# Values of two mixers computed in feature layout and turned by TensorE transposes, and a denominator summed in two fp32r parts

## The chip, the cores and the metric

The kernel runs on one core of one Trainium2 chip. The metric is the device time of one execution in microseconds (us), lower is better. Before the change the median of 3 runs is 1262.3 us (1262.03 to 1263.04).

## The reference

One layer of a decoder: 512 tokens and 16 learned meta tokens in front of them (528 in all), width 1024, all in float32. One input projection feeds three token mixers; this change touches the values of two of them and a denominator of the second.

```python
z = xn @ p["w_in"] + p["b_in"]          # 528 x 9696: q, k, v, r, a of GLA; DSA; q, k, v, o, i, f of mLSTM; gates
# GLA, 4 heads, keys 128 wide, values 256 wide, chunks of tokens:
o = einsum("bhtk,bhkv->bhtv", q * exp(G), S) + einsum("bhts,bhsv->bhtv", A, v)
# mLSTM, 4 heads, the same widths:
num = w_inter * einsum("bhtk,bhkv->bhtv", q, Cs) + einsum("bhts,bhsv->bhtv", P, v)
den = w_inter * einsum("bhtk,bhk->bht", q, ns) + sum(P, axis=-1)
h = num / maximum(abs(den), exp(-m))
# both: rms_norm per head, times a gate, then a projection to 1024
mix = sigmoid(gate_a) * y_a + sigmoid(gate_b) * y_b + sigmoid(gate_c) * y_c
h = h + rms_norm(mix @ p["w_out"], p["g_post_mix"])
h = h + rms_norm(square(relu(rms_norm(h, g) @ p["w_up"])) @ p["w_down"], p["g_post_mlp"])
```

## The kernel before

**Three products for one.** A product with a weight matrix is done on TensorE in the type fp32r. Activations and weights are split into a rounded part and a rest (`xh` and `xl`, `whi` and `wlo`), and three products are summed: high by high, high by low, low by high. A weight chunk is 1024 rows by 128 columns. SyncE loads it to one of three buffers `wraw`; GpSimd splits it to one of four buffers `whi`/`wlo` (L620, L624); TensorE uses it. `plan()` lists the chunks and the tiles that TensorE makes of them, in the order in which it makes them.

**Tiles and slots.** A tile of a product goes to one of two slots `GP` of PSUM, in turn. The next tile in a slot waits on the semaphore `gfree` until VectorE or ScalarE has copied the last one out. A tile in *feature layout* has its 128 channels on the partitions and the tokens along the free axis: the weight chunk is the stationary operand, the tokens stream. With `both=True` it covers all 528 tokens in two streams of 264 (L1871), otherwise 512 tokens (L1874). So 24 or 48 matmuls make a tile.

**Values before.** The mixers need values with tokens on the partitions. So the values of a head are made in *token layout*: 128 tokens are the stationary operand, and 256 columns of two weight chunks stream (L1889). Tile A has token tiles 0 and 1, tile B has 2 and 3, with 48 matmuls each. 16 tokens are left over: the first ones for GLA, the last ones for mLSTM. They are made in tile M by 16 matmuls (L1880, L1881), whose stationary operand `xm` holds the high and the low part of these tokens side by side in 32 columns. VectorE copies the tiles to `vh` (L1393) and `vm` (L1398) and adds the bias, which lies in `vb` on all partitions.

**Order of the work.** Every engine's queue is written out by hand. TensorE's main loop goes over the heads. Small steps of head h (`level`, `weighted`, `scores`, `recalled`, `squares`) stand between tiles for head h+1 (`nxt(...)`), so that TensorE has matrix work while VectorE and ScalarE prepare the next small step. In GLA the order per head is: tile gq of head h+1, `squares` of head h-1, gk, seven `level` steps with gg, gr, gr and A between them, the transposes of the keys (L2237, L2239), half of B, the state matmuls (L2244, L2247), the other half, M, `weighted` (L2188). In mLSTM it is: mq, `squares`, mq, `scores` 0 and 1 (L2285), mk, `scores` 2 and 3, A, `recalled` (L2293, L2294), the sum for the denominator, B, M. In the last head of each mixer, gate tiles (`ta`, `tc`) stand where the next head's tiles would.

**Denominator before.** VectorE adds the four weight blocks `AT` into `Wd` (L1697 to L1701, semaphore `sum_w`). TensorE multiplies a matrix of ones with `AT` for the first 112 columns (L2324) and with `Wd` for the other 400 (L2326), in plain fp32, which takes two instructions each. VectorE takes it up in `denominator` (L1707).

Of the kernel before, what the change touches and what calls it, by code (L numbers as in the profile page):

```python
# [69 lines left out]
def _rows():  # L70
    at = 0
    for name, n, src in [
        ("gq", 4, "b_in"), ("gk", 4, "b_in"), ("gr", 8, "b_in"), ("cq", 2, "b_in"), ("ckv", 1, "b_in"),
        ("ik", 1, "b_in"), ("mq", 4, "b_in"), ("mk", 4, "b_in"), ("mo", 8, "b_in"), ("gate", 24, "b_in"),
        ("a2", 4, "b_gla_a"), ("hg", 2, "g_gla_head"),
        ("hm", 2, "g_ml_head"), ("dq", 2, "g_dsa_q"), ("dkv", 1, "g_dsa_kv"), ("ig", 1, "idx_ln_g"),
        ("ib", 1, "idx_ln_b"), ("fb", 1, "ml_f_bias"), ("cv", 32, "ml_conv"),
    ]:
        ROWS[name] = at
        ROW_LIST.append((name, n, src))  # L80
        at += n
    return at
# [6 lines left out]
JOINED = {"gq": 8, "cq": 3, "mq": 8}  # L89
FOLLOWS = ("gk", "ckv", "mk")  # L90
# [21 lines left out]
NROWDMA = 22  # L112
# [22 lines left out]
def plan():  # L135
# [89 lines left out]
    def all_values(name, c0):  # L225
        pad()
        values(name, c0)

    gla(0)
    all_values("gv0", C_GV)  # L230
    for h in range(HEADS):
# [5 lines left out]
        if h + 1 < HEADS:  # L237
            all_values(f"gv{h + 1}", C_GV + (h + 1) * DV)
# [52 lines left out]
def build(nc, a, line, scratch, rows, out):  # L291
# [3 lines left out]
    with ctx:  # L295
# [6 lines left out]
        def region(offset, specs):  # L302
# [23 lines left out]
        xm = sb("xm", [P, KT, 2 * META], F32R)  # L326
# [44 lines left out]
        (sgate, gtmp, vb, qh, ATm, kh, vh, vm, AT, sqo, rso, on, km) = region(AO, [  # L371
            ("sgate", [P, 2, SEQ], FP32), ("gtmp", [P, 2, SEQ], FP32), ("vb", [P, D], FP32),
# [3 lines left out]
        BO = AO + (2 * SEQ * 2 + D + 2 * SEQ + 2 * ALL + 2 * QT * DV + 2 * DV + QT * SEQ + SEQ + 2 * SEQ + SEQ + 2 * SEQ + 2 * P) * 4  # L376
# [7 lines left out]
        (zc, cv, sgc, lf_, bcum_, M_, uT, uTt, fbias_, um_, Mb, Md, Wd, Mt, Wt, ATt, later_t) = region(BO, [  # L384
# [244 lines left out]
        def _(act):  # L629
# [41 lines left out]
            def input_high(t):  # L671

                if t == QT:
# [172 lines left out]
            act.dma_start(vb[:, :], a["b_in"][0:1, C_GV:C_GV + D].broadcast_to([P, D])).then_inc(ld_a, 16)  # L846
# [81 lines left out]

            gate_of(0)
            for h in range(HEADS):  # L930
                last = h == HEADS - 1
                level(h, 0)
                if h:
                    squared(h - 1)
                level(h, 1)
# [4 lines left out]
                level(h, 2)  # L940
                if last:
# [39 lines left out]
            act.dma_start(vb[:, :], a["b_in"][0:1, C_MV:C_MV + D].broadcast_to([P, D])).then_inc(ld_v, 16)  # L981
# [64 lines left out]
            fetch_maxima(0)  # L1046
            def head_squares(h):
# [10 lines left out]
            for h in range(HEADS):  # L1058
# [15 lines left out]
                floor_of(h)  # L1074
                if more:
# [7 lines left out]
                if more:  # L1083
                    conv_sig(h + 1, 1)
# [94 lines left out]
        def _(dve):  # L1179
# [45 lines left out]
            def input_low(t):  # L1225
                if t == QT:
# [3 lines left out]
                    dve.wait_ge(xl_ok, KT + 1)  # L1230
                    nc.vector.tensor_copy(xm[:, :, META:2 * META], xl[:, :, 0:META].bitcast(FP32)).then_inc(xl_ok, 1)
# [1223 lines left out]
```

## Time and profile before

| what | value |
|---|---|
| median of 3 runs | 1262.3 us |
| profiled execution, its own time | 1262.05 us |
| its span, first to last instruction | 1260.1 us |
| TensorE (PE) busy | 1252.5 us, 99%, 6561 instructions |
| VectorE (DVE) busy | 629.7 us, 50% |
| ScalarE (ACT) busy | 392.7 us, 31% |
| GpSimd (POOL) busy | 771.8 us, 61% |
| granted TensorE clock, mean | 0.999 |

The GLA heads run from about 345 to 560 us, the mLSTM heads from about 633 to 790 us of the span. The duration of a matmul in a row is from its start to its modelled end, and neighbours overlap: what a matmul costs is the distance from its start to the next start. In the table of groups a duration is a mean; in the timeline `xN` joins N neighbours that are alike.

### The profile page before, as it was taken

Reading aid. Unit: us, or ns where it says so; the run is one execution under the profiler, and the core shown is the slowest. Engines: PE = TensorE matmul, PEld = TensorE weight load, DVE = VectorE, ACT = ScalarE, POOL = GpSimd, SP = SyncE. Lnnn points to the kernel's source line nnn. Section 1 sums busy time; section 2 is a strip of 40 time slices with the busy share of each in tenths; the row PEclk is TensorE's granted clock in tenths of the full one; section 3 lists DMA queues with packets and bytes.
Section 4 is the critical chain, followed back from the end, with each engine's and each line's share of the span. In section 5 each row is a group of like instructions: output and inputs, shape, how many; then the busy total and the mean of one; then the engine's idle time right before and its main releaser. Section 6 shows DMA issues by size and latency. Waiting matters only on the chain.

```text
span 1260.1 us, 17438 instructions
## 1 busy us (share of the span) xinstructions
PE 1252.5 (99%) x6561; PEld 1028.6 (82%) x6564; DVE 629.7 (50%) x1115; ACT 392.7 (31%) x810; POOL 771.8 (61%) x914
## 2 busy tenths in 40 slices
PE   9999999999999999999999999999999999999998
PEld 8866887677899899888899987887888888888886
DVE  4368887642276786835446773342511112333434
ACT  5343555533013333333024343312511111221322
POOL 8746430225574753758775556784876676888882
PEclk9999999999999999999999999999999999999999
DMA  6846200323331321322443333522333333232221
GB/s 176 253 123 212 68 2 25 80 56 94 84 84 51 84 68 51 84 68 84 118 117 77 87 90 100 195 89 85 84 101 101 86 99 108 93 101 84 100 84 67
DMA packets 167433, 120.08 MB, mean 95 GB/s; under 512 B 11367, under 2 KB 145613, under 8 KB 167350
## 3 DMA queue, kind: packets, MB, share of 16 engines
q1 hardware_dynamic: 160612, 107.79, 29.7%
q10 hardware_dynamic: 6738, 11.18, 2.7%
q8 instruction: 52, 0.85, 0.3%
q14 instruction: 31, 0.25, 0.1%
HBM read 114.71 MB, written 9.62 MB: 99 GB/s over the span
## 4 chain that ended last, share of the span: by engine, by line
PE 99%; ACT 0%; DVE 0%; issue 0%; DVEq 0%; ACTq 0%
PE GP L1874 46%; PE GP L1910 9%; PE PA L1910 9%; PE GP L1889 7%; PE GP L1871 6%; PE PA L2075 3%; PE GP L2137 3%; PE PA L2175 1%; PE PA L2112 1%; PE PA L2293 1%; PE GP L2368 1%; PE GP L1956 1%; PE PA L2045 1%; PE PA L2285 1%; PE PA L2076 1%; PE GP L1881 1%
## 5 line engine op out<-in xcount | busy, mean ns | idle before, releaser
L624 POOL TENSOR_TENSOR wlo<-wraw,whi 128x256 fp32r<-128x256 f32 x708 | 563.9, 827 | 14.8
L620 POOL TENSOR_SCALAR whi<-wraw 128x1024 fp32r<-128x1024 f32 x177 | 201.0, 1135 | 449.2 <-PE GP L1874 226.6
L1874 PE MATMUL GP<-xh,whi 128*128 128x512 f32 x352 | 144.8, 411 | 0.0
L1874 PE MATMUL GP<-xh,wlo 128*128 128x512 f32 x352 | 139.0, 395 | 0.0
L1874 PE MATMUL GP<-xl,whi 128*128 128x512 f32 x352 | 138.8, 394 | 0.0
L1816 DVE TENSOR_TENSOR ul<-U,uh 128x512 fp32r<-128x512 f32 x64 | 65.3, 1055 | 109.4 <-ACT uh L1158 109.4
L1874 PE MATMUL GP<-nh,whi 128*128 128x512 f32 x240 | 95.1, 396 | 0.0
L1874 PE MATMUL GP<-nl,whi 128*128 128x512 f32 x240 | 95.1, 396 | 0.0
L1874 PE MATMUL GP<-nh,wlo 128*128 128x512 f32 x240 | 95.1, 396 | 0.0
L1820 DVE SCALAR_TENSOR_TENSOR U<-GP,rrow 128x512 f32<-128x512 f32 x32 | 22.1, 692 | 141.7 <-PE GP L1874 140.3
L1874 PEld LDWEIGHTS GP<-xh,whi 128*128 128x128 f32 x352 | 66.3, 188 | 16.0 <-issue 1.5
L1874 PEld LDWEIGHTS GP<-xh,wlo 128*128 128x128 f32 x352 | 66.1, 188 | 15.3
L1874 PEld LDWEIGHTS GP<-xl,whi 128*128 128x128 f32 x352 | 66.3, 188 | 14.3 <-issue 0.5
L1158 ACT ACTIVATE uh<-U 128x512 fp32r<-128x512 f32 x64 | 37.2, 625 | 129.0 <-PE PA L1910 70.4
L1874 PE MATMUL GP<-yh,whi 128*128 128x512 f32 x192 | 76.3, 397 | 0.0
L1874 PE MATMUL GP<-yl,whi 128*128 128x512 f32 x192 | 76.1, 396 | 0.0
L1874 PE MATMUL GP<-yh,wlo 128*128 128x512 f32 x192 | 76.1, 396 | 0.0
L1889 PE MATMUL GP<-whi,xh 128*128 128x256 f32 x256 | 74.6, 292 | 0.2 <-DVE kh L1404 0.2
L1889 PE MATMUL GP<-wlo,xh 128*128 128x256 f32 x256 | 71.9, 281 | 0.0
L1889 PE MATMUL GP<-whi,xl 128*128 128x256 f32 x256 | 71.7, 280 | 0.0
L1162 ACT ACTIVATE U<-U 128x512 f32<-128x512 f32 x32 | 20.2, 632 | 152.9 <-DVE U L1820 152.9
L1874 PEld LDWEIGHTS GP<-nh,wlo 128*128 128x128 f32 x240 | 45.2, 188 | 11.0
(426 smaller groups left out, 2770.5 us busy)
## 6 DMA issues: line engine op xcount, KB each, us to landing
wraw<-in_w_in SPq DMA_DIRECT2D x75, 512.0 KB, 3.9
wraw<-in_w_up SPq DMA_DIRECT2D x32, 512.0 KB, 4.0
wraw<-in_w_down SPq DMA_DIRECT2D x32, 512.0 KB, 3.5
line_rows<-bias_line SPq DMA_DIRECT2D x8, 655.0 KB, 5.2
table<-line_rows SPq DMA_DIRECT2D x4, 1024.0 KB, 5.7
wraw<-in_w_br_dsa SPq DMA_DIRECT2D x8, 512.0 KB, 4.3
wraw<-in_w_br_gla SPq DMA_DIRECT2D x8, 512.0 KB, 4.0
wraw<-in_w_br_ml SPq DMA_DIRECT2D x8, 512.0 KB, 4.0
```

The costliest lines, as they stand in the source:

```text
L620: nc.gpsimd.tensor_scalar(hi, src, 1.0, 1.0, ALU.mult, ALU.mult).then_inc(hi_done, 1)
L624: part = nc.gpsimd.tensor_tensor(lo[:, at:to], src[:, at:to], hi[:, at:to].bitcast(FP32), ALU.subtract)
L1158: nc.scalar.activation(uh[:, k % 4, :], U[:, k % FT, :], ACT.Copy).then_inc(uh_ok, 1)
L1162: nc.scalar.activation(U[:, m, :], U[:, m, :], ACT.Square).then_inc(U_ok, 1)
L1816: tt(ul[:, k % 4, :], U[:, k % FT, :], uh[:, k % 4, :].bitcast(FP32), ALU.subtract).then_inc(ul_ok, 1)
L1820: stt(U[:, m, :], ps[:, 0:SEQ], 0.0, rrow[:, :], ALU.max, ALU.mult).then_inc(gfree[tl[f"up{m}"].slot], 1)
L1871: ins = mm(ps[0:t.m, b * SEQ:b * SEQ + HALF], wt[:, s0, w], hx[:, k, b * HALF:(b + 1) * HALF], start=st, stop=sp_)
L1874: ins = mm(ps[0:t.m, 0:SEQ], wt[:, s0, w], av, start=st, stop=sp_)
L1889: ins = mm(o_, at_[:, k, tok], wt[:, s0:s0 + 2, k * P:(k + 1) * P], start=(k == 0 and p_ == 0), stop=(k == KT - 1 and p_ == 2))
L1910: ins = mm(accumulators(name, hf, i), av[:, i * P:(i + 1) * P], wt[:, c["hl"], k * SEQ:(k + 1) * SEQ], start=(n == 0 and k == 0 and p_ == ...
L2075: mm(bank(v % 2)[0:r, 0:w], qlat[:, h, TILE_AT[i]:TILE_AT[i + 1]], kvT[:, 0:w], start=True, stop=False)
L2137: ins = mm(pairs_of(o_, g), kvn[:, j, :], pairs_of(PT[:, g % 2, j, :], g), start=(j == 0), stop=(j == i))
```

## The change

1. `plan()`: a head's values are two feature tiles of all 528 tokens, `gv{h}0` and `gv{h}1` (`mv{h}0`, `mv{h}1`), one weight chunk each, 48 matmuls each. Tiles A, B and M are gone, and so are `xm`, its four copies, `vb` and the two DMAs that filled it.
2. ScalarE copies such a tile to `vT` and adds the bias (`value_in`). TensorE turns it with five transposes into a tile `T0` or `T1` of its own (`turned`): four of 128 tokens and one of the 16 left over. In GLA VectorE copies T0 (`values`) and ScalarE copies T1 (`values_copied`) to `vh` and `vm`; in mLSTM VectorE copies both.
3. The denominator's sum is split in two fp32r parts: ScalarE writes the rounded part (`sum_hi`), VectorE the rest (`weight_rest`, `sum_lo`), and TensorE sums each with one matmul of 512 columns over `onesr`.
4. Fewer and longer DMAs of biases (20 for 22).

```diff
@@ plan
-    def values(name, c0):
-        c = [chunk("w_in", c0, P), chunk("w_in", c0 + P, P)]
-        tile(name + "A", c, 0, kind="V", off=0)
-        tile(name + "B", c, 0, kind="V", off=2)
-        tile(name + "M", c, 2, kind="VT" if name[0] == "m" else "VM")
+    def turned(name, v):
+        tile(f"{name}T{v}", [], 0, kind="T")
+    def value(name, c0, h, v):
+        feature(f"{name}{h}{v}", "w_in", c0 + (2 * h + v) * P, both=True)
@@ ScalarE
+            def value_in(name, h, v):
+                if h:
+                    act.wait_ge(gemm_done, tl[f"{name}{h - 1}T{v}"].val)
+                t = tl[f"{name}{h}{v}"]
+                nc.scalar.activation(two(vT[:, v, :]), halves(ready(f"{name}{h}{v}")), ACT.Identity,
+                                     bias=cc(name, 2 * h + v)).then_inc(gfree[t.slot], 1)
             gate_of(0)
+            value_in("gv", 0, 0)
+            value_in("gv", 0, 1)
             for h in range(HEADS):
                 level(h, 0)
                 if h:
                     squared(h - 1)
+                    values_copied(h)
@@ ScalarE, mLSTM
                 floor_of(h)
+                act.wait_ge(sum_w, h + 1)
+                for c, s_ in WSUM:
+                    ins = nc.scalar.activation(Wr[:, 1, c], s_[:, c], ACT.Copy)
+                ins.then_inc(sum_hi, 1)
...
                 out_gate(h, 1)
                 if more:
+                    value_in("mv", h + 1, 0)
                     conv_sig(h + 1, 1)
...
                 head_squares(h)
+                if more:
+                    value_in("mv", h + 1, 1)
@@ VectorE
+            def values(name, h, v):
+                ps, c = ready(f"{name}{h}T{v}"), slice(v * P, (v + 1) * P)
+                nc.vector.tensor_copy(vh[:, h % 2, :, c], ps[:, 0:SEQ].rearrange("p (t n) -> p t n", t=QT))
+                nc.vector.tensor_copy(vm[0:META, h % 2, c], ps[0:META, SEQ:SEQ + P]).then_inc(gfree[...], 1)
+            def weight_rest(h):
+                dve.wait_ge(sum_hi, h + 1)
+                for c, s_ in WSUM:
+                    ins = tt(Wr[:, 0, c], s_[:, c], Wr[:, 1, c].bitcast(FP32), ALU.subtract)
+                ins.then_inc(sum_lo, 1)
...
                 weight_sums(h)
                 if more:
                     conv(h + 1, 0)
+                weight_rest(h)
@@ TensorE
+                elif t.kind == "T":
+                    evacuated(name[0:3] + name[4])
+                    for i in range(QT):
+                        nc.tensor.transpose(ps[:, i * P:(i + 1) * P], vT[:, v, first + i * P:first + (i + 1) * P], ident[:, :])
+                    ins = nc.tensor.transpose(ps[0:META, SEQ:SEQ + P], vT[:, v, few], ident[:, :])
...
                 nxt("gq")
                 if h:
                     squares(h - 1)
+                else:
+                    gemm("gv0T0")
                 nxt("gk")
+                if h == 0:
+                    gemm("gv0T1")
...
-                nxt("gvB", 1)
-                nxt("gvM")
+                nxt("gv1", 1)
+                nxt("gvT0")
                 pe.wait_ge(od_q, 6 * h + 6)
                 weighted(h).then_inc(av_ps, 1)
+                if h + 1 < HEADS:
+                    gemm(f"gv{h + 1}T1")
...
                 scores(h, 1)
+                gemm(f"mv{h}T1")
                 nxt("mk")
...
-                mm(bank(3)[:, 0:FROM[1]], ones[:, :], AT[:, 0, 0:FROM[1]], start=True, stop=True)
-                pe.wait_ge(sum_w, h + 1)
-                mm(bank(3)[:, FROM[1]:SEQ], ones[:, :], Wd[:, 0, FROM[1]:SEQ], start=True, stop=True).then_inc(av_ps, 1)
-                nxt("mvB")
-                nxt("mvM")
+                pe.wait_ge(sum_lo, h + 1)
+                mm(bank(3), onesr[:, :], Wr[:, 1, :], start=True, stop=False)
+                mm(bank(3), onesr[:, :], Wr[:, 0, :], start=False, stop=True).then_inc(av_ps, 1)
+                nxt("mvT0")
+                nxt("mv1")
```

How TensorE's queue changes, at two places. The first is GLA head 0, where the last matmuls of tile gq of head 1 (`xh,whi` 128x512) meet the first of its gk (128x264). Before:

```order
L1874 MATMUL GP<-xh,whi 128x512
L1874 MATMUL GP<-xl,whi 128x512
L1874 MATMUL GP<-xh,wlo 128x512
L1871 MATMUL GP<-xh,whi 128x264 [waits split_done,gfree0]
L1871 MATMUL GP<-xh,whi 128x264
L1871 MATMUL GP<-xl,whi 128x264 x2
L1871 MATMUL GP<-xh,wlo 128x264 x2
```

And with the change (the same lines of code are L1900 and L1897 there, the transposes L1906 and L1907):

```order
L1900 MATMUL GP<-xh,whi 128x512
L1900 MATMUL GP<-xl,whi 128x512
L1900 MATMUL GP<-xh,wlo 128x512
L1906 MATMUL GP<-ident,vT 128x128 [waits gfree0,gfree1]
L1906 MATMUL GP<-ident,vT 128x128 x3
L1907 MATMUL GP<-ident,vT 16x128
L1897 MATMUL GP<-xh,whi 128x264 [waits split_done,gfree0]
L1897 MATMUL GP<-xh,whi 128x264
L1897 MATMUL GP<-xl,whi 128x264 x2
```

T0 has come between gq and gk. It takes a slot, so gk now goes to the slot of gq and waits for the copy of gq itself; before, it waited for a tile older than that. The second place is mLSTM head 0, from the last `recalled` matmuls over the sum to the next tile. Before:

```order
L2293 MATMUL PA<-AT,vh 128x144
L2294 MATMUL PA<-ATt,vm 128x16
L2324 MATMUL PA<-AT,ones 128x112
L2326 MATMUL PA<-Wd,ones 128x400 [waits sum_w]
L1889 MATMUL GP<-whi,xh 128x256 [waits split_done,gfree1]
L1889 MATMUL GP<-wlo,xh 128x256
L1889 MATMUL GP<-whi,xl 128x256
```

With the change:

```order
L2314 MATMUL PA<-AT,vh 128x144
L2315 MATMUL PA<-ATt,vm 128x16
L2349 MATMUL PA<-Wd_r,onesr 128x512 [waits sum_lo]
L2350 MATMUL PA<-Wd_r,onesr 128x512
L1906 MATMUL GP<-ident,vT 128x128 [waits gfree1,gfree0]
L1906 MATMUL GP<-ident,vT 128x128 x3
L1907 MATMUL GP<-ident,vT 16x128
L1897 MATMUL GP<-xh,whi 128x264 [waits split_done,gfree1]
L1897 MATMUL GP<-xh,whi 128x264
```

The sum now waits on `sum_lo`, the last of three steps on VectorE, ScalarE and VectorE, where it waited on the first of them. Behind it stands T0 of the next head instead of tile B.

## Rows read from the trace of the kernel before

**Rows 1.** The page: busy us of each engine, share of the span, instructions.

```profile
PE 1252.5 (99%) x6561; PEld 1028.6 (82%) x6564; DVE 629.7 (50%) x1115; ACT 392.7 (31%) x810; POOL 771.8 (61%) x914
```

**Rows 2.** Waits of TensorE, two of four: us in total, times, longest.

```profile
PE PA L1931 <- DVE ones L1203: 1.2, 1, 1.2
...
PE GP L1889 <- DVE kh L1404: 0.2, 1, 0.2
```

**Rows 3.** Timeline, PE, mLSTM start: start us, us, engine line op out<-in xcount.

```profile
621.38 0.40 PE L1871 MATMUL GP<-xh,whi 128*128 128x264 f32 x2
...
633.05 0.28 PE L1889 MATMUL GP<-whi,xh 128*128 128x256 f32 x1
...
644.36 0.28 PE L1880 MATMUL GP<-whi,xm 128*32 128x256 f32 x1
...
646.21 0.40 PE L1871 MATMUL GP<-xh,whi 128*128 128x264 f32 x2
```

**Rows 4.** Timeline, PE: eight transposes early in the kernel.

```profile
16.64 1.03 PE L1924 MATMUL PA<-ident,X 128*128 128x128 f32 x8
17.43 0.48 PE L1956 MATMUL GP<-xh,wlo 128*128 128x256 f32 x2
```

**Rows 5.** Timeline, PE: four transposes of keys in GLA head 0.

```profile
391.14 0.41 PE L1889 MATMUL GP<-whi,xh 128*128 128x256 f32 x1
...
394.00 0.28 PE L1889 MATMUL GP<-whi,xl 128*128 128x256 f32 x1
394.26 0.30 PE L2237 MATMUL PA<-ident,km 128*128 128x128 f32 x1
...
397.56 0.59 PE L2244 MATMUL PA<-vm,AT 128*128 128x256 f32 x2
```

**Rows 6.** Timeline, DVE: the copy of `km` that these transposes wait for.

```profile
393.93 0.18 DVE L1198 COPY km<-KHt 128x32 f32<-128x32 f32 x1
```

**Rows 7.** Timeline, PE: the denominator's sum in mLSTM head 0, the next tile.

```profile
670.80 0.45 PE L2324 MATMUL PA<-AT,ones 128*128 128x112 f32 x2
...
671.89 0.28 PE L1889 MATMUL GP<-wlo,xh 128*128 128x256 f32 x1
```

**Rows 8.** Timeline, PE: an fp32r sum over `onesr` between two halves of mq.

```profile
682.19 0.40 PE L2197 MATMUL PA<-sqr,onesr 128*128 128x512 f32 x1
...
682.66 0.40 PE L1871 MATMUL GP<-xh,whi 128*128 128x264 f32 x2
```

**Rows 9.** Timeline, ACT and DVE, GLA head 0: from the first level to the copy of gq.

```profile
361.81 0.63 ACT L864 ACTIVATE E<-E 128x512 f32<-128x512 f32 x1 [14.09 <-DVE E L1442]
...
366.24 0.74 DVE L1401 TENSOR_SCALAR qg<-GP,col 128x512 f32<-128x512 f32 x1
```

**Rows 10.** Timeline, PE and ACT: `scores`, copy of mq, mk; gate of the output.

```profile
685.58 0.59 PE L2285 MATMUL PA<-qh,kh 128*128 128x512 f32 x1
685.77 0.70 ACT L989 ACTIVATE zc<-GP,col 128x528 f32<-128x528 f32 x1 [1.21 <-PE GP L1871]
...
686.80 0.59 PE L1871 MATMUL GP<-xh,whi 128*128 128x264 f32 x1
...
701.59 1.14 ACT L1040 ACTIVATE sgate<-sgate 128x512 f32<-128x512 f32 x2
```

**Rows 11.** Timeline, DVE and ACT, mLSTM head 1: weight sums, convolution, sigmoid, `sqr`.

```profile
696.64 0.59 DVE L1701 TENSOR_TENSOR Wd<-Wd,ATt 16x16 f32<-16x16 f32 x1
...
697.68 2.74 DVE L1661 SCALAR_TENSOR_TENSOR cv<-zc,col,cv 128x528 f32<-128x528 f32 x3
...
700.45 0.64 ACT L997 ACTIVATE sgc<-cv 128x528 f32<-128x528 f32 x1 [7.67 <-DVE cv L1661]
...
710.23 0.69 DVE L1717 TENSOR_TENSOR sqr<-sqo,sqr 128x512 fp32r<-128x512 f32 x1
```

**Rows 12.** Timeline, PE, mLSTM: a sum, and the matmul that waits for `sqr`.

```profile
704.35 0.45 PE L2324 MATMUL PA<-AT,ones 128*128 128x112 f32 x2
...
715.75 0.40 PE L2197 MATMUL PA<-sqr,onesr 128*128 128x512 f32 x1
```

More of the change, by code:

```diff
@@ L237, in plan @@
         if h + 1 < HEADS:
-            all_values(f"gv{h + 1}", C_GV + (h + 1) * DV)
+            value("gv", C_GV, h + 1, 0)
+            value("gv", C_GV, h + 1, 1)
+            turned(f"gv{h + 1}", 0)
+            turned(f"gv{h + 1}", 1)
     gates("ta", C_GATE, 2, 8)
@@ L244, in plan @@
     feature("mk0", "w_in", C_MK, both=True)
-    all_values("mv0", C_MV)
+    value("mv", C_MV, 0, 0)
+    value("mv", C_MV, 0, 1)
     for h in range(HEADS):
-        if h + 1 < HEADS:
+        more = h + 1 < HEADS
+        if more:
             feature(f"mq{h + 1}", "w_in", C_MQ + (h + 1) * DK, both=True)
+        else:
+            gates("tc", C_GATE + 2 * D, 0, 1)
+        if h == 0:
+            turned("mv0", 0)
+        turned(f"mv{h}", 1)
+        if more:
             feature(f"mk{h + 1}", "w_in", C_MK + (h + 1) * DK, both=True)
-        else:
-            gates("tc", C_GATE + 2 * D, 0, 2)
-        if h + 1 < HEADS:
-            all_values(f"mv{h + 1}", C_MV + (h + 1) * DV)
+            value("mv", C_MV, h + 1, 0)
+            turned(f"mv{h + 1}", 0)
+            value("mv", C_MV, h + 1, 1)
+        else:
+            gates("tc", C_GATE + 2 * D, 1, 2)
     gates("tc", C_GATE + 2 * D, 2, 8)
@@ L940, in _ @@
                 level(h, 2)
+                if h == 0:
+                    values_copied(0)
                 if last:
@@ L956, in _ @@
                 off_out(h)
+                if not last:
+                    value_in("gv", h + 1, 0)
                 sigmoids(h)
+                if not last:
+                    value_in("gv", h + 1, 1)
                 if last:
-                    whole("gv3M")
                     gate_in("ta", 0, 3)
@@ L1046, in _ @@
             fetch_maxima(0)
+            value_in("mv", 0, 0)
+            value_in("mv", 0, 1)
             def head_squares(h):
@@ L1088, in _ @@
                 head_squares(h)
+                if more:
+                    value_in("mv", h + 1, 1)
             gate_in("tc", 16, 3)
-            whole("mv3M")
             gate_in("tc", 16, 4)
@@ L1553, in _ @@
             forget_sums(0)
-            for part in range(3):
-                values("gv", 0, part)
             for h in range(HEADS):
@@ L1728, in _ @@
             dve.wait_ge(ml_c, 2)
-            dve.wait_ge(ld_v, 16)
-            for part in range(3):
-                values("mv", 0, part)
             for h in range(HEADS):
@@ L1736, in _ @@
                     head_scaled(h - 1)
+                else:
+                    values("mv", 0, 0)
                 for j in range(2):
                     weights_of(h, j)
+                values("mv", h, 1)
                 if h:
@@ L1754, in _ @@
                 head_sums(h)
-                if more:
-                    for part in range(1, 3):
-                        values("mv", h + 1, part)
             head_scaled(HEADS - 1)
@@ L2201, in _ @@
             gemm("gk0")
-            pe.wait_ge(ld_a, 48)
+            pe.wait_ge(ld_a, 32)
             pe.wait_ge(gla_c, 2)
-            for nm in ("gg0", "gv0A", "gv0B", "gv0M"):
+            for nm in ("gg0", "gv00", "gv01"):
                 gemm(nm)
@@ L2217, in _ @@
                     squares(h - 1)
+                else:
+                    gemm("gv0T0")
                 nxt("gk")
+                if h == 0:
+                    gemm("gv0T1")
                 level(h, 0)
@@ L2312, in _ @@
                     pe.wait_ge(av_rs, HEADS + h)
+                else:
+                    gemm("mv0T0")
                 scores(h, 0)
                 scores(h, 1)
+                gemm(f"mv{h}T1")
                 nxt("mk")
```

123 lines of the change are left out of this document (46 added, 77 removed).

## The prediction, made before the changed kernel was run

> **What bounds the kernel now.** I read the page first: TensorE is busy 99% of the span; no other engine is over 61% [rows 1]. The second view is the list of TensorE's waits. It has four rows, of which two are shown [rows 2]; the other two are 0.2 us each, so TensorE waits 1.8 us in all, and only 0.2 us of that lies in the part that changes. So TensorE's own queue is the time: every instruction taken from it or added to it counts in full, and a wait that the change brings counts too, since there is no slack under it. The third view is the timeline of TensorE. A matmul's printed duration overlaps the next one's, so I price everything by the distance from start to start. The fourth is the timeline of ScalarE and VectorE around the places where TensorE will now wait for them.
>
> **The change part by part, on TensorE.**
>
> Tile M goes. It runs from 644.36 to 646.21 [rows 3], 1.85 us, and there are 8 (4 heads, 2 mixers): -14.8 us.
>
> Tiles A and B become two feature tiles. A and B take 644.36 - 633.05 = 11.31 us, two tiles in the new form (mq0 and mk0) 633.05 - 621.38 = 11.67 us [rows 3], since they stream 264 columns, not 256: +0.36 for each of 8 heads, +2.9 us.
>
> 80 transposes come, in 16 tiles of five. Eight transposes take 17.43 - 16.64 = 0.79 us [rows 4]. The 17.43 row has two matmuls in 0.48 us, where one of 0.28 and a normal start-to-start distance of 11.31/96 = 0.12 would make 0.40, so the first one behind the transposes costs 0.08 more. That is 0.87 us for eight, 0.109 each, 0.54 for a tile: +8.7 us. From both sides: the keys' transposes are the dearest row. From 391.14 to 397.56 [rows 5] lie 6.42 us with two half tiles (48 matmuls, 5.66 us) and four transposes; that leaves 0.76 us. Part of it is a wait: the last matmul before starts at 394.00 and the transposes at 394.26, 0.14 more than the normal 0.12, and the copy they wait for ends at 394.11 [rows 6]. If all of 0.76 - 0.14 = 0.62 were the transposes', they would cost 0.155 each, 0.78 a tile, 12.4 us in all, 3.7 more than I take. The cheapest is five at 0.09, 0.45 a tile, if the drain that I add is hidden by the fp32 step that often follows: 1.5 less. I take 0.54, because its row has no wait in it.
>
> The denominator. From L2324 at 670.80 to the second matmul of the next tile at 671.89 are 1.09 us [rows 7]; less a normal 0.12, the sum costs 0.97. The new form stands in [rows 8]: two fp32r matmuls over `onesr` take 682.66 - 682.19 = 0.47, plus 0.08 of restart after an fp32 step, 0.55. So -0.42 in each of 4 heads: -1.7 us.
>
> The wait for `km` in [rows 5, 6] shrinks, as the half tile ahead of it becomes 0.36/4 = 0.09 longer: -0.3 us over GLA heads 0 to 2.
>
> **What TensorE will wait for.** A turning is short, so a tile that follows one has little cover. A tile's copy costs about 0.2 us until ScalarE starts (685.58 to 685.77) and 0.70 for the copy itself [rows 10]; VectorE's of gq takes 0.74 [rows 9].
>
> In GLA head 0, gk now waits for the copy of gq, and only T0 (0.54) lies between them. Is VectorE free in time? ScalarE's first level exponential is queued behind both `value_in` copies and so starts 0.2 + 0.7 = 0.9 us after the second value tile. From that exponential to the copy of gq VectorE needs 366.24 - 361.81 = 4.43 us [rows 9], 5.3 together. The gq tile takes 24 matmuls of 0.47/2 = 0.235 us [rows 8], 5.6, so VectorE just makes it. Then the copy costs 0.2 + 0.74 + 0.05 = 1.0 against 0.54 of cover: +0.5 us, once. Queued behind it are all of head 0's tiles. If the wait hit an already late VectorE it would grow by up to the chain's margin of 0.3.
>
> In mLSTM, mk waits for mq's copy, done at 685.77 + 0.70 = 686.47, and mk starts at 686.80 [rows 10]; T1 now stands between and moves mk to 687.3. Slack 0.8. T0 waits for `value_in`, which ScalarE starts after the output gates, 701.59 + 1.14 = 702.7, and ends at 703.4, while TensorE comes at 704.35 + 0.47 = 704.8 [rows 10, 12]. Slack 1.4. `sum_lo`: the weight sums end at 696.64 + 0.59 = 697.2, ScalarE is idle (7.67 us before 700.45, [rows 11]) and makes the rounded part in about 1 us under the convolution, which ends at 700.42 [rows 11]; two subtractions of together 0.9 us (an estimate from VectorE's 0.69 for 512 columns [rows 11] and a start) end at 701.3; TensorE comes at 704.35 [rows 12]. Slack 3.0. Last, `sqr` ends at 710.92 [rows 11] and is wanted at 715.75 [rows 12]. VectorE's chain grows by 1.0 us, TensorE arrives 1.85 + 0.2 - 0.54 = 1.5 us earlier (M and part of the sum gone, T0 come): slack 4.8 - 2.5 = 2.3. In the other GLA heads `weighted` lies between a value tile's end and its T1: 32 instructions of 128 columns, 3.5 us if each takes a transpose's 0.109 (an estimate). So I count nothing for these.
>
> The bias DMAs and the copies for `xm` are on no engine that TensorE waits for [rows 2]: 0. GpSimd splits the same chunks; they are freed one by one instead of by pairs, and TensorE never waits for it [rows 2]: 0.
>
> **Sum.** -14.8 + 2.9 + 8.7 - 1.7 - 0.3 + 0.5 = -4.7 us. The profiled execution took 1262.05 us (span 1260.1 and 1.95 around it), so 1257.35 for such a one; it lies 0.25 under the median of the runs, so 1257.6.
>
> **The rivals.**
>
> A, transposes at the dear price. The 0.155 us each of [rows 5] gives -4.7 + 3.7 = -1.0, so 1261.3: no change that can be told. For it: half of the new tiles stand directly behind or before fp32r matmuls, as the keys' do. Against: the keys' row contains a wait, and [rows 4] does not.
>
> B, slower: the handover around turnings. The mechanism is the one at gk: a turning covers 0.54 us, the copy it or its neighbour waits for costs 1.0. At one of 16 tiles nothing else lies between, by the queue. If ScalarE and VectorE come late at the others too, each costs 0.5: 15 x 0.5 = 7.5, so 1257.6 + 7.5 = 1265.1. It decides from a mean wait of 4.7/15 = 0.3 us per turning. For it: four of the slacks above are 0.8 us or so, and ScalarE executes in order, so one late step moves all of them. Against: every slack is positive, and ScalarE is 31% busy [rows 1].
>
> C, the sum's parts come late. It needs 3.0 us of delay on the way over ScalarE and back to VectorE; if they came 2 us behind TensorE in three heads: +6, 1263.6. Against: ScalarE's idle 7.67 us at that place [rows 11].
>
> D, transposes one after another. If each held TensorE for its printed duration, 0.30 us [rows 5], instead of 0.109, then 80 x 0.19 = 15.3 more: 1272.9. Against: the eight of [rows 4] occupy 0.79 us, start to start. The Trainium skill, page "TensorE: Matmul & The Clock Gate", section "Part 4: PE-mode transpose", gives about 275 ns for a 128x128 transpose in a kernel and calls TensorE's access latency the larger part of it; by that rule a turning would cost 1.4 us and the change would lose. The trace agrees with it as a duration and not as a distance between neighbours.
>
> E, cheaper: the drains are hidden and gk's wait does not come: -4.7 - 1.5 - 0.5 = -6.7, 1255.6.
>
> **How the numbers follow.** The forecast's own range is 1256.4 to 1259.7, chance 0.60; A 0.15 (half of its cases between 1259.8 and 1261, counted as no change); B 0.08; C 0.03; D 0.01; E 0.13. A measurement of this kernel can tell about 0.2% from no change, 2.5 us, so faster is below 1259.8: forecast, E, and a little of A, 0.75. Within 0.2%: most of A and the mild cases of B, 0.17. Slower: 0.08. The range takes in E with half a us more on its far side and all of A: 1255.0 to 1261.5.
>
> **What would show it.** In the timeline after: two value tiles of about 5.83 us; five transposes and the restart in about 0.54; gk of head 1 about 0.5 us behind T0's end, with VectorE's `qg` as its releaser; the sum in 0.47; no wait longer than 0.2 us on `Wd`, `vT` or `zc`; TensorE still 99%. Wrong it would be if the list of waits named ScalarE's `vT` or VectorE's `vh` many times (B), `Wd_r` (C), or if five transposes took 0.8 us or more (A).

## The result and the profile after

The changed kernel takes 1264.89 us (median of 20 runs, 1263.99 to 1265.61); the kernel before, beside it, 1263.09 us (20 runs, 1261.93 to 1264.02). The ratio is 1.0015, interval 1.0009 to 1.0022: a little slower, where 1257.6 us (1255.0 to 1261.5) was forecast. The profiled execution took 1265.57 us, its span is 1263.6. The page after, in the form of [rows 1]:

```profile
PE 1250.2 (99%) x6505; PEld 1026.8 (81%) x6508; DVE 625.9 (50%) x1120; ACT 407.5 (32%) x841; POOL 774.1 (61%) x914
```

TensorE is busy 2.3 us less, in a span 3.5 us longer, so waits came. The sum of busy time hides part of the work that went: the matmuls behind a wait last longer (0.50 us and not 0.40 for the squares below), and in e2, where the new waits are gone, TensorE is busy 4.5 us less than before (1248.0 against 1252.5). The list of TensorE's waits after (us in total, times, longest), which stands against [rows 2]:

```profile
PE PA L2306 <- ACT rso L653: 2.8, 3, 1.3
PE PA L2214 <- DVE sqr L1745: 2.8, 2, 1.5
PE PA L1948 <- DVE ones L1237: 1.2, 1, 1.2
PE GP L1897 <- DVE qg L1427: 0.3, 1, 0.3
```

The first two are new: 5.6 us, all in mLSTM; the fourth is the one that the forecast expected at gk; three more of 0.2 us each are not shown. L2214 is the product that sums the squares of a finished head, L2306 the first product of the next head's `scores`, which waits for the head's root. The forecast's own prices can be read on TensorE's timeline, mLSTM head 0 (start us, us, engine line, operation):

```profile
651.21 0.60 PE L1906 MATMUL GP<-ident,vT 128*128 128x128 f32 x4
651.64 0.27 PE L1907 MATMUL GP<-ident,vT 128*16 128x128 f32 x1
651.75 1.70 PE L2306 MATMUL PA<-qh,kh 128*128 128x512 f32 x4
...
671.28 0.48 PE L2349 MATMUL PA<-Wd_r,onesr 128*128 128x512 f32 x1
671.60 0.39 PE L2350 MATMUL PA<-Wd_r,onesr 128*128 128x512 f32 x1
671.83 0.60 PE L1906 MATMUL GP<-ident,vT 128*128 128x128 f32 x4
```

A turning costs 651.75 - 651.21 = 0.54 us, as forecast; the sum 671.83 - 671.28 = 0.55, as forecast.

**Where the waits come from.** GpSimd's timeline over the end of mLSTM head 1, first in the kernel before (in brackets: idle before it, and its releaser):

```profile
694.39 3.85 POOL L624 TENSOR_TENSOR wlo<-wraw,whi 128x256 fp32r<-128x256 f32 x4
713.17 1.87 POOL L620 TENSOR_SCALAR whi<-wraw 128x1024 fp32r<-128x1024 f32 x1 [14.92 <-PE GP L1881]
715.12 2.83 POOL L624 TENSOR_TENSOR wlo<-wraw,whi 128x256 fp32r<-128x256 f32 x4
```

and in the changed one:

```profile
700.19 1.29 POOL L629 TENSOR_SCALAR whi<-wraw 128x1024 fp32r<-128x1024 f32 x1 [1.79 <-PE GP L1897]
701.57 4.52 POOL L633 TENSOR_TENSOR wlo<-wraw,whi 128x256 fp32r<-128x256 f32 x4
711.95 1.49 POOL L629 TENSOR_SCALAR whi<-wraw 128x1024 fp32r<-128x1024 f32 x1 [5.86 <-PE GP L1897]
713.53 4.19 POOL L633 TENSOR_TENSOR wlo<-wraw,whi 128x256 fp32r<-128x256 f32 x4
```

Before, both value slots came free only when tile M was done, so GpSimd lay idle for 14.92 us (698.24 to 713.17), and just then VectorE runs the chain of instructions that ends in `sqr`, the squares of the finished head. Now each slot comes free with its own tile, and GpSimd splits on top of that chain. VectorE's timeline there, changed kernel:

```profile
700.50 1.11 DVE L1728 TENSOR_TENSOR Wd_r<-AT,Wd_r 128x112 fp32r<-128x112 f32 x1
...
702.01 2.35 DVE L1566 TENSOR_TENSOR yl<-on,yh 128x512 fp32r<-128x512 f32 x2
704.29 1.21 DVE L1693 SCALAR_TENSOR_TENSOR qh<-cv,sgc 128x512 f32<-128x512 f32 x1
...
712.57 1.42 DVE L1743 SCALAR_TENSOR_TENSOR sqo<-gtmp,sqo 128x512 f32<-128x512 f32 x1
714.02 0.84 DVE L1744 CAST sqr<-sqo 128x512 fp32r<-128x512 f32 x1
714.89 1.09 DVE L1745 TENSOR_TENSOR sqr<-sqo,sqr 128x512 fp32r<-128x512 f32 x1
```

`sqr` ends at 715.98, 5.06 us after [rows 11], where the forecast had 1.0; 0.16 of the 5.06 is the distance of the two traces at the start of the weight sums (694.54 and 694.38). TensorE and ScalarE behind it:

```profile
716.04 0.50 PE L2214 MATMUL PA<-sqr,onesr 128*128 128x512 f32 x1 [1.33 <-DVE sqr L1745]
...
720.87 1.46 PE L2306 MATMUL PA<-qh,kh 128*128 128x512 f32 x3 [1.15 <-ACT rso L653]
```

```profile
717.87 0.31 ACT L1043 ACTIVATE Wt<-Mt,uTt 32x16 f32<-32x16 f32 x1 [4.86 <-DVE Mt L1702]
...
719.59 0.57 ACT L652 ACTIVATE rso<-PA 128x512 f32<-128x512 f32 x1
720.19 0.63 ACT L653 ACTIVATE rso<-rso 128x512 f32<-128x512 f32 x1
```

So one delay costs twice: `sqr` is late for the squares (1.33 us), and `Mt`, soon behind it on VectorE, is late for the decays, behind which the root stands in ScalarE's queue (1.15 us).

### The profile page after: what moved, and what is told of

It reads as the page before. It is cut to its first block, busy times and chain, and to the rows that moved or that the text cites. A ratio compares the mean times of both kernels' runs of the same rounds, so it can differ in the third digit from the quotient of the medians.

```text
span 1263.6 us, 17359 instructions
## 1 busy us (share of the span) xinstructions
PE 1250.2 (99%) x6505; PEld 1026.8 (81%) x6508; DVE 625.9 (50%) x1120; ACT 407.5 (32%) x841; POOL 774.1 (61%) x914
## 4 chain that ended last, share of the span: by engine, by line
PE 93%; DVE 5%; ACT 2%; issue 1%; DVEq 0%; ACTq 0%
PE GP L1900 45%; PE GP L1897 10%; PE GP L1927 9%; PE PA L1927 9%; PE PA L2092 3%; PE GP L2154 3%; PE PA L2192 1%; PE PA L2129 1%; DVE cv L1682 1%; PE GP L2392 1%; PE GP L1973 1%; PE PA L2062 1%; PE PA L2306 1%; PE PA L2093 1%; PE PA L2205 1%; PE PA L2206 1%
## 5 line engine op out<-in xcount | busy, mean ns | idle before, releaser
L633 POOL TENSOR_TENSOR wlo<-wraw,whi 128x256 fp32r<-128x256 f32 x708 | 576.8, 845 | 14.7
L629 POOL TENSOR_SCALAR whi<-wraw 128x1024 fp32r<-128x1024 f32 x177 | 189.7, 1072 | 450.5 <-PE GP L1900 250.2
L1900 PE MATMUL GP<-xh,whi 128*128 128x512 f32 x352 | 144.7, 411 | 0.0
L1900 PE MATMUL GP<-xl,whi 128*128 128x512 f32 x352 | 139.4, 396 | 0.0
L1900 PE MATMUL GP<-xh,wlo 128*128 128x512 f32 x352 | 139.3, 396 | 0.0
L1897 PE MATMUL GP<-xh,whi 128*128 128x264 f32 x480 | 101.6, 293 | 0.5 <-DVE qg L1427 0.3
L1897 PE MATMUL GP<-xl,whi 128*128 128x264 f32 x480 | 97.6, 285 | 0.0
L1897 PE MATMUL GP<-xh,wlo 128*128 128x264 f32 x480 | 97.2, 284 | 0.0
L1900 PE MATMUL GP<-nh,whi 128*128 128x512 f32 x240 | 95.0, 396 | 0.0
L1900 PE MATMUL GP<-nl,whi 128*128 128x512 f32 x240 | 95.0, 396 | 0.0
L1900 PE MATMUL GP<-nh,wlo 128*128 128x512 f32 x240 | 95.0, 396 | 0.0
L1900 PEld LDWEIGHTS GP<-xh,whi 128*128 128x128 f32 x352 | 66.4, 189 | 16.0 <-issue 1.5
L1900 PEld LDWEIGHTS GP<-xh,wlo 128*128 128x128 f32 x352 | 66.2, 188 | 15.4
L1900 PEld LDWEIGHTS GP<-xl,whi 128*128 128x128 f32 x352 | 66.5, 189 | 13.9 <-issue 0.5
L1897 PEld LDWEIGHTS GP<-xh,whi 128*128 128x128 f32 x480 | 75.0, 189 | 3.3 <-issue 1.4
L1900 PE MATMUL GP<-yh,whi 128*128 128x512 f32 x192 | 76.2, 397 | 0.0
L1900 PE MATMUL GP<-yl,whi 128*128 128x512 f32 x192 | 76.0, 396 | 0.0
L1900 PE MATMUL GP<-yh,wlo 128*128 128x512 f32 x192 | 76.0, 396 | 0.0
L1897 PEld LDWEIGHTS GP<-xl,whi 128*128 128x128 f32 x480 | 74.7, 188 | 0.0
```

The costliest lines, as they stand in the source:

```text
L629: nc.gpsimd.tensor_scalar(hi, src, 1.0, 1.0, ALU.mult, ALU.mult).then_inc(hi_done, 1)
L633: part = nc.gpsimd.tensor_tensor(lo[:, at:to], src[:, at:to], hi[:, at:to].bitcast(FP32), ALU.subtract)
L1897: ins = mm(ps[0:t.m, b * SEQ:b * SEQ + HALF], wt[:, s0, w], hx[:, k, b * HALF:(b + 1) * HALF], start=st, stop=sp_)
L1900: ins = mm(ps[0:t.m, 0:SEQ], wt[:, s0, w], av, start=st, stop=sp_)
```

## The experiments

Three theories. **Theory 1**: collision; a VectorE instruction with two SBUF inputs is held up by a GpSimd split beside it. **Theory 2**: VectorE's list is simply longer by the two new subtractions, and TensorE comes 1.5 us earlier. **Theory 3**: ScalarE's order, in which the root stands behind the decays, makes the scores late.

**e1_hold_next and e2_hold_pair.** Only the moment changes at which a value slot may be overwritten. In e2:

```diff
+    for h in range(HEADS):
+        chunks[tiles[f"mv{h}0"].chunks[0]]["end"] = tiles[f"mv{h}1"].val
     real, held = [], [None] * NHL
```

In e1 both chunks of a head get the value of the tile behind them instead (`mq{h + 1}`, or `tc0`).

> The changed kernel, with one thing altered: GpSimd may overwrite the slots of both mLSTM value chunks only once the next tile behind them (query of the next head, or the first tc gate) is done, so its splitting falls behind VectorE's chain and not beside it. Theory 1 (collision: splits beside VectorE's denominator and sum chain make its instructions with two SBUF inputs some 0.5 us longer each): the yl subtractions of heads 1 and 2 go back from 1.2 to about 0.7 us each, the last sqr subtraction from 1.1 to 0.7; TensorE's waits for sqr and for the root fall from 5.6 us to under 2; time 1259 to 1261, below the kernel before. Theory 2 (the chain is only longer by its two new subtractions and TensorE comes 1.5 us earlier): the waits stay within 1 us of 5.6 and the time within 1 us of the changed kernel's 1264.9. Theory 3 (ScalarE's order, root behind decays and value copies): the wait for the root (2.8) stays, the one for sqr may go: 1262 to 1263.

> The changed kernel, but the first mLSTM value chunk's slot is released together with the second's, as pairs were before; the second split still starts while VectorE sums squares. Theory 1: only the first of two collisions goes (yl and qh, some 1.5 us a head in heads 0 to 2), so about half or more of the 5.6 us: time 1261 to 1263. Theory 2: no change, 1264 to 1266. Theory 3: the wait for the root stays, 1263 to 1265.

e1: 1259.50 us (8 runs), ratio 0.9976, interval 0.9966 to 0.9986. e2: 1257.32 us (5 runs), ratio 0.9957, interval 0.9943 to 0.9970. e1 lies in the forecast of theory 1; e2 lies 4 us below its own (1261 to 1263). In e2 both new waits are gone from the list. VectorE's chain in e2:

```profile
698.87 0.27 DVE L1730 TENSOR_TENSOR Wd_r<-AT,Wd_r 128x112 fp32r<-128x112 f32 x1
...
699.54 1.28 DVE L1568 TENSOR_TENSOR yl<-on,yh 128x512 fp32r<-128x512 f32 x2
700.74 0.68 DVE L1695 SCALAR_TENSOR_TENSOR qh<-cv,sgc 128x512 f32<-128x512 f32 x1
...
708.25 0.69 DVE L1745 SCALAR_TENSOR_TENSOR sqo<-gtmp,sqo 128x512 f32<-128x512 f32 x1
708.97 0.43 DVE L1746 CAST sqr<-sqo 128x512 fp32r<-128x512 f32 x1
709.43 0.69 DVE L1747 TENSOR_TENSOR sqr<-sqo,sqr 128x512 fp32r<-128x512 f32 x1
```

and the next split and the squares there:

```profile
710.32 1.31 POOL L631 TENSOR_SCALAR whi<-wraw 128x1024 fp32r<-128x1024 f32 x1 [13.54 <-PE GP L1899]
```

```profile
712.91 0.40 PE L2216 MATMUL PA<-sqr,onesr 128*128 128x512 f32 x1
```

From `Wd_r` to the end of `sqr` the chain takes 15.48 us in the changed kernel and 11.25 in e2. The steps shown account for 0.84 + 1.07 + 0.53 + 0.73 + 0.41 + 0.40 = 3.98 of the 4.23, and a convolution step (0.75 against 0.49) for the rest. I had expected e2's second split to stay beside `sqr`; but a chain that isn't held up at 700 is over at 710.12, before that split starts. In e1 the four splits lie so late that they reach the next head's chain: `yl` stays at a mean of 1.04 us (1.04 in the changed kernel too, 0.68 in e2), while `sqr` is back at 0.69; TensorE still waits 0.6 us for it. Theory 2 as the whole cause falls: nothing in VectorE's list was altered.

**e9_root_first and e10_hold_root_first.** ScalarE takes the root ahead of the first two decays, alone and with e2's release.

```diff
+                if h:
+                    head_root(h - 1)
                 decay(h, 0)
                 decay(h, 1)
-                if h:
-                    head_root(h - 1)
```

> The changed kernel, with ScalarE taking the head's root before the next head's first two decays and not behind them. Theory 3 (ScalarE's order is what makes the scores late): the wait for the root, 2.8 us, vanishes, and the time falls by 2 to 3 us, to 1262 to 1263. Theory 1: the squares stay late by 2.8 us, and what the root gains of 1.1 us a head the decays lose, as VectorE's weights now wait for them: 1264 to 1267.

> e2_hold_pair with ScalarE's root ahead of the decays, as in e9_root_first: both cures together. If the collision is the cause and the root's place only passes its delay on (theory 1), nothing is left for the root's place to win: 1257.3 within 0.5 us. If the root's place has a price of its own (theory 3), the 3.4 us that it gained in e9_root_first come again in part: 1256 or less.

e9: 1261.49 us (11 runs), ratio 0.9985 (0.9977 to 0.9994). My theory's number was wrong and theory 3's too low a gain: the wait for the root is gone, that for `sqr` (2.8) unchanged, and the decays lose nothing, since they run beside VectorE's two `on` products. e10: 1257.67 us (5 runs), against e2's 1257.32: nothing left to win. So the root's place is a second link of the same chain: it doubles a delay and makes none.

**e5_zero_low.** GpSimd writes zeros for the low part of the mLSTM value weights, which leaves that part of the product out.

```diff
+                if c["src"] == "w_in" and c["c0"] is not None and C_MV <= c["c0"] < C_MV + D:
+                    nc.gpsimd.memset(lo.bitcast(FP32), 0.0).then_inc(split_done, 1)
+                    continue
```

> The changed kernel, with the low part of the mLSTM value weights left out: GpSimd writes zeros there and reads nothing, in place of four subtractions of 1.1 us each; the rounding pass of 1.3 us before it stays, at the same points of time. Theory 1: yl and qh fall from 1.2 to about 0.7 us, sqo's and sqr's steps partly; waits for sqr and root from 5.6 to under 2.5 us, time 1259 to 1262. Theory 2: 1264 to 1266. If writing alone blocks VectorE as well, the overlap is only shorter and the time in between.

1260.73 us (10 runs), ratio 0.9981 (0.9972 to 0.9990), inside the forecast of theory 1. GpSimd, then VectorE, at the first collision:

```profile
698.39 1.29 POOL L629 TENSOR_SCALAR whi<-wraw 128x1024 fp32r<-128x1024 f32 x1 [1.78 <-PE GP L1900]
699.74 0.95 POOL L632 MEMSET wlo<- 128x1024 f32 x1
```

```profile
698.70 1.11 DVE L1731 TENSOR_TENSOR Wd_r<-AT,Wd_r 128x112 fp32r<-128x112 f32 x1
699.73 0.56 DVE L1731 TENSOR_TENSOR Wd_r<-Wd,Wd_r 128x400 fp32r<-128x400 f32 x1
700.22 1.28 DVE L1569 TENSOR_TENSOR yl<-on,yh 128x512 fp32r<-128x512 f32 x2
```

The second `Wd_r` stands wholly beside the memset (699.74 to 700.69), the first `yl` for 0.5 us of it, and both take what they take undisturbed (0.57 and 1.28 in e2). Beside the rounding pass, which reads, the first `Wd_r` is still held. The 2.8 us of waits that are left (1.5 and 1.3) come at the end of head 2, where the splits beside the chain are those of gate weights, which this edit leaves alone.

**e12_round_pieces.** The rounding pass as four instructions of 256 columns.

```diff
-                nc.gpsimd.tensor_scalar(hi, src, 1.0, 1.0, ALU.mult, ALU.mult).then_inc(hi_done, 1)
+                for at in range(0, n, PIECE):
+                    to = min(at + PIECE, n)
+                    part = nc.gpsimd.tensor_scalar(hi[:, at:to], src[:, at:to], 1.0, 1.0, ALU.mult, ALU.mult)
+                part.then_inc(hi_done, 1)
```

> The changed kernel, with GpSimd's rounding pass of a chunk (1.05 us for 1024 columns) issued as four of 256 columns, as its subtractions are. Asked is how VectorE is held up. If a VectorE instruction waits until the GpSimd instruction under way has ended, the subtraction of 112 columns that stands at 1.11 us under the rounding pass falls to 0.4 to 0.6, the sqo step from 1.42 to about 1.0, and the time to 1263 to 1264.5. If both share a bandwidth all the while, the durations and the time stay (1264.9 within 0.4).

1261.75 us (11 runs), ratio 0.9992 (0.9983 to 1.0000), 3.1 us under the changed kernel and more than I expected. VectorE there:

```profile
698.94 0.47 DVE L1731 TENSOR_TENSOR Wd_r<-AT,Wd_r 128x112 fp32r<-128x112 f32 x1
...
700.02 1.68 DVE L1569 TENSOR_TENSOR yl<-on,yh 128x512 fp32r<-128x512 f32 x2
...
710.62 0.77 DVE L1746 SCALAR_TENSOR_TENSOR sqo<-gtmp,sqo 128x512 f32<-128x512 f32 x1
```

The hold-up follows the length of GpSimd's instruction, so these rows speak for a wait for its end and against a shared bandwidth, under which the durations should have stayed. The wait for `sqr` is gone; 1.8 us for the root stay. GpSimd pays: its rounding pass takes 1.51 us undisturbed, not 1.04, and 2.78 beside this chain. Waits of 1.4 us for `wlo` are new, all outside the mLSTM heads; that the slower pass causes them is likely and not tested.

**e6_before_collide and e11_sum_collide.** The other way round: in the kernel before, and in the kernel before with the new denominator, the splits are laid on the chain by the release alone.

```diff
+    for h in range(1, HEADS):
+        for c in ("mq", "mk"):
+            chunks[tiles[f"{c}{h}"].chunks[0]]["end"] = tiles[f"mv{h}A"].val
     real, held = [], [None] * NHL
```

> The kernel before, with no arithmetic or order changed: the slots of the mLSTM query and key chunks are released only when tile A of the values behind them is done, so that GpSimd's two splits of 4 to 5 us, which stand at 688 to 698 us in head 1, fall on 701 to 710, beside VectorE's chain, where GpSimd idles before. Theory 1 (collision): yl, qh, conv and kh there get up to 0.5 us longer each, 2.5 to 4 us in all per head against a slack of 2.3; waits for sqr or the root appear on TensorE, and the time is 1264 to 1268, 2 to 5 us above the kernel before. Theory 2 (a longer instruction list on VectorE is what made the changed kernel late): nothing changes, 1262 to 1264, and the durations stay at 0.68.

> e4_sum_only (the kernel before with the new denominator alone) with the release of e6_before_collide, which laid GpSimd's splits beside the chain and made sqr 1.3 us later in head 2 without a wait. Slack is what is disputed: e6_before_collide used 1.3 us of it, the new denominator 0.9 us more on VectorE while TensorE comes 0.4 us a head earlier. If the sum passes the slack, waits for sqr or the root of 0.3 to 1 us a head show up and the gain of 1.6 us shrinks: 1261.8 to 1263.5. If the two do not add up (theory 2: only the list's length counts), it is e4_sum_only's 1261.3 within 0.4.

e6: 1263.86 us (11 runs), ratio 1.0005 (0.9996 to 1.0014): no difference that can be told, so the number that I gave theory 1 was missed. The longer durations did come (`qh` and three convolution steps; 0.68 and 2.38 undisturbed):

```profile
700.04 1.52 DVE L1675 SCALAR_TENSOR_TENSOR qh<-cv,sgc 128x512 f32<-128x512 f32 x1
...
702.48 3.42 DVE L1664 SCALAR_TENSOR_TENSOR cv<-zc,col,cv 128x528 f32<-128x528 f32 x3
...
711.55 0.69 DVE L1720 TENSOR_TENSOR sqr<-sqo,sqr 128x512 fp32r<-128x512 f32 x1
```

From `yl` to the end of `sqr` lie 712.24 - 698.84 = 13.40 us against 710.92 - 700.34 = 10.58 before: 2.8 longer, in the 2.5 to 4 that I forecast. But `yl` starts 1.5 earlier, because the splits that I moved away had stood beside the weight sums, so `sqr` ends only 1.3 later. And the 2.3 of slack in my forecast is the changed kernel's; the kernel before has 715.75 - 710.92 = 4.8 ([rows 11, 12]).

e11: 1270.58 us (5 runs), ratio 1.0058 (1.0045 to 1.0071), far above both forecasts. What gives way here is a tighter slack than that of `sqr`: VectorE's copy of value tile B is queued behind `sqr`, and TensorE's next tile needs the slot. In the kernel before the copy ends at 711.88 and that tile starts at 712.84, right behind tile M; in e6 they stand at 712.84 and 713.10, with 0.28 in place of 0.12 behind M's last matmul. With the two subtractions on top the copy comes too late. Waits, then TensorE's timeline at one, then its granted clock in windows (us; PE, PEld, DVE, ACT, POOL busy; PEclk; DMA share; GB/s):

```profile
PE GP L1889 <- DVE vh L1403: 3.1, 2, 2.8
PE GP L1892 <- DVE vh L1403: 2.8, 1, 2.8
```

```profile
716.38 0.78 PE L1889 MATMUL GP<-xh,whi 128*128 128x264 f32 x2 [2.83 <-DVE vh L1403]
...
717.84 0.64 PE L1889 MATMUL GP<-xh,whi 128*128 128x264 f32 x2
718.28 0.64 PE L1889 MATMUL GP<-xl,whi 128*128 128x264 f32 x2
...
720.00 0.40 PE L1889 MATMUL GP<-xh,whi 128*128 128x264 f32 x2
720.24 0.41 PE L1889 MATMUL GP<-xl,whi 128*128 128x264 f32 x2
```

```profile
717.40:718.40 1.00, 1.00 (x6) 1.00 (x6) 0.33 (x1) 0.55 (x3) 1.00 (x3) 0.50 0.00 0
...
720.40:721.40 1.00, 1.00 (x8) 0.91 (x8) 0.00 (x0) 0.01 (x1) 1.00 (x2) 1.00 0.88 247
```

**e3_old_sum, e4_sum_only, e8_hold_old_sum, e7_hold_both.** e3 and e8 are the changed kernel and e2 with the old denominator; e4 is the kernel before with the new one; e7 is e2 with the same release for GLA's value chunks too. In e3 and e8 ScalarE's copies and VectorE's `weight_rest` go as well, in e4 they come; shown is TensorE's part in e3 and e8, and e4 is the other way round.

```diff
-                pe.wait_ge(sum_lo, h + 1)
-                mm(bank(3), onesr[:, :], Wr[:, 1, :], start=True, stop=False)
-                mm(bank(3), onesr[:, :], Wr[:, 0, :], start=False, stop=True).then_inc(av_ps, 1)
+                mm(bank(3)[:, 0:FROM[1]], ones[:, :], AT[:, 0, 0:FROM[1]], start=True, stop=True)
+                pe.wait_ge(sum_w, h + 1)
+                mm(bank(3)[:, FROM[1]:SEQ], ones[:, :], Wd[:, 0, FROM[1]:SEQ], start=True, stop=True).then_inc(av_ps, 1)
```

> The changed kernel with the old denominator: two fp32 products with ones, no copies by ScalarE, no subtractions by VectorE. TensorE gets 1.7 us more work. Theory 1: the chain is 0.9 to 1.7 us a head shorter (the two subtractions, of which one collides), so the waits fall from 5.6 to 3 to 4 us, and the time comes out within 0.6 us of the changed kernel's. Theory 2: the waits vanish but for the copies' 0.3, and the time is 2 to 4 us below the changed kernel's: 1261 to 1263.

> The kernel before with only the new denominator: the rounded part by ScalarE, the rest by VectorE, two fp32r products. Value tiles as before, so GpSimd idles while the chain runs. Theory 1: the chain gets 0.9 us a head longer without collision and stays within its slack of 2.3 us: waits as before (1.8 us), time 1.7 us under the kernel before, 1261.0 to 1261.8. Theory 2: the chain is late by itself, waits for sqr or the root of 1 us or more appear, and the time is the kernel before's within 0.5 us or above it.

> The changed kernel with the pairs' release of e2_hold_pair and with the old denominator: what the denominator in two parts is worth once nothing collides. Theory 1: TensorE is the bound again, so the full 1.7 us of work come back: 1258.6 to 1259.4 against 1257.3 of e2_hold_pair. Theory 2 (chain length decides): the two kernels are equal or this one is faster, under 1257.5.

> The changed kernel with the pairs' release of e2_hold_pair in the GLA heads as well as in the mLSTM heads. Theory 1: in GLA TensorE waits for VectorE in head 0 alone (0.5 us), so there is nothing to win: 1257.3 within 0.4 us. If collisions in GLA cost something that the waits don't show, the time is 1256.5 or less; if GpSimd's later start makes TensorE wait for weights there, 1258 or more.

| value tiles | old denominator | new denominator | new - old |
|---|---|---|---|
| as before | 1262.88 | 1261.32 (e4, 11 runs) | -1.6 |
| new, slots released one by one | 1262.49 (e3, 11 runs) | 1264.89 (the change) | +2.4 |
| new, released by pairs | 1259.44 (e8, 7 runs) | 1257.32 (e2) | -2.1 |

Ratios to the kernel before: e4 0.9986 (0.9978 to 0.9995), e3 0.9997 (0.9988 to 1.0006), e8 0.9970 (0.9959 to 0.9982). The medians were taken at several times, and the kernel before, measured beside each, lay between 1262.88 and 1263.12; so much may be added to a difference. The same denominator wins 1.6 to 2.1 us where nothing collides with the chain and loses about 2.4 in the changed kernel. e4 and e8 came out as theory 1 had it (e8 at the edge). e3 did not: its time is the one that theory 2 forecast, 2.4 us under the changed kernel, though not all its waits vanish (2.5 us for the root; e8 has none). So theory 2 has this much right: the longer list counts, but only with the collision that eats the slack. e7: 1257.85 us (5 runs), 0.9958 (0.9945 to 0.9970), 0.5 above e2 and a little outside my 0.4: nothing won, so the collisions in GLA cost no time that this shows.

## Why the prediction was wrong

The step that failed is one sentence: GpSimd "splits the same chunks; they are freed one by one instead of by pairs, and TensorE never waits for it [rows 2]: 0". Both halves are true, and the 0 doesn't follow. TensorE waits for VectorE, and VectorE for GpSimd. The term measures 1264.89 - 1257.32 = 7.6 us. Start to start the changed kernel falls back against e2 by 7.0 us in mLSTM heads 1 to 3 (787.48 - 779.52 at their end, 651.21 - 650.22 ahead of them), at the squares and scores only. The list has 5.6 for these places; the rest is the longer first matmuls behind each wait.

- **The sum of work**, -4.7: right within a microsecond. With the collision away (e2) it is -5.6 between the medians. Its parts: the turnings 0.54 each and the sum 0.55 as forecast; the tiles -3.4 (e8; -3.6 against the kernel before as measured beside it, 1263.03) against the -3.0 of -14.8 + 2.9 + 8.7 - 0.3 + 0.5; the denominator -1.6 to -2.1 against -1.7. That e2's 1257.32 lies 0.3 beside the forecast of 1257.6 is partly luck: the work is 0.9 better than forecast, and the median of 3 runs that it was counted from is 0.6 below that of the 24 beside e2.
- **gk's wait**, +0.5: right. T0 starts at 365.03 and gk at 366.03, 0.46 more than a turning; the list shows 0.3 of it, for `qg`.
- **The slack of `sqr`**, 2.3: right as far as it goes. In e2 `sqr` ends at 710.12 and TensorE comes at 712.91, 2.8 later. All its durations came from [rows 11], where GpSimd stands still from 698.24 on; with GpSimd beside it the chain is 4.2 longer, and the slack becomes 1.33 of wait. The trace of the kernel before had the price elsewhere. In mLSTM head 0, where a split stands beside the same three convolution steps, they take 3.45 us, and 2.38 at 702.89, where GpSimd is idle:

```profile
628.66 4.29 POOL L624 TENSOR_TENSOR wlo<-wraw,whi 128x256 fp32r<-128x256 f32 x4
628.90 3.45 DVE L1661 SCALAR_TENSOR_TENSOR cv<-zc,col,cv 128x528 f32<-128x528 f32 x3
```

- **The root**: not looked at. It stands behind the decays in ScalarE's queue and so passes VectorE's delay to `scores` (e9).
- **The rivals**: none held this. B, 1265.1, was the nearest in time and wrong in place, so its nearness is luck: of the copies at turnings only `qg` is waited for. A and D are refuted by the 0.54 of a turning, C by the list of waits, which holds none for `Wd_r`. E's cheaper transposes did not show either. B's argument that four of the slacks are 0.8 or so was misread: of the slacks worked out for mLSTM (0.8, 1.4, 3.0, 2.3) one is.

The Trainium skill, page "SBUF — State Buffer", section "Who interferes with whom", had the rule: a VectorE instruction with two SBUF inputs contends with a GpSimd instruction that reads SBUF, not with one that only writes it, and the one that comes second waits until the first has ended. The trace agrees in each part: `Wd_r` at 1.11 beside the rounding pass (0.27 alone), ending 0.13 us behind it (701.61 and 701.48); the second `Wd_r` undisturbed beside the memset of e5; 0.47 when the pass is cut in four. The page names copies and casts too, where their operands allow a mode that uses both ports, and the cast of `sqr` goes from 0.43 to 0.84.

## What to carry to other kernels

When a change moves the moment at which a buffer comes free, follow it to the engine that refills it, and ask which instructions of a third engine it will now stand beside; an idle stretch of GpSimd beside a critical VectorE chain can be what keeps that chain short. Take slack from durations only if the neighbours stay as they were. And in an in-order queue look at what stands behind the late instruction: here a chain late by one delay cost twice, and the cure was a release held back by one tile (e2, 1257.32 us, the lowest median here; e7 and e10 lie 0.3 to 0.5 above it).

## What was not expected of the hardware

- GpSimd pays as well: beside the chain its four subtractions take 4.52 us instead of 2.81 to 2.83, the rounding pass 1.29 to 1.49 instead of 1.05. VectorE's instructions that read PSUM keep their time beside a split (in e11 `gtmp` from `PA` 0.68, while `kh`, from two SBUF inputs, takes 1.15 and not 0.71).
- Two delays don't add up linearly: 1.3 us of hold-up (e6) and two subtractions (e4, 1.6 us faster) add no wait alone; together they cost 9.3 us over e4 (e11). 5.9 of that are the waits, about 2.8 are slower matmuls, 1.4 behind each of the two long waits. Behind a wait of 2.83 us, the granted clock is 0.50 (1.2 GHz of 2.4) in three stretches of a microsecond (716.4 to 719.4), a pair of matmuls of 264 columns takes 0.44 us from start to start instead of 0.24, and then the clock is back at 1.00. The half tile there takes 4.34 us (716.38 to 720.72) where the next one, at full clock, takes 2.92 (721.19 to 724.11). Behind the changed kernel's waits of 1.15 to 1.45 us no such drop shows: the granted clock stays at 1.00.
- The first 20 us differ by up to 1.6 us between the profiled executions: the eight transposes of [rows 4], at 16.64, start at 18.23 in the changed kernel. How much of that belongs to a kernel and how much to an execution stays open; the profiled execution of the kernel before (1262.05) lay 0.8 under the median of its 24 later runs, and the changed kernel's (1265.57) 0.7 over its own. So the terms here are taken from medians, or from distances within one trace.
